# Attention value products with the values as weights, and the softmax division moved ahead of the transposes

## The reference, cut to what matters

```
# sparse attention (branch a)
logits = einsum('bqhd,bqkhd->bhqk', qb, k_sel) * scale
p = softmax(where(valid, logits, -inf))
y_a = einsum('bhqk,bqkhd->bqhd', p, v_sel)
# stick-breaking attention (branch c)
a = where(strict, exp(log_beta + later), 0.0)
y_c = einsum('bhqs,bshd->bqhd', a, v)
# every branch n, then the output
merged += gates[n] * (branches[n] @ w_branch[n])
return merged @ w_out
```

## Time and profile before

| | |
|---|---|
| median of 3 timed runs | 885.44 us (884.88 to 887.35) |
| span of the profiled execution | 883.3 us |
| outside the span (median less span) | 2.1 us |
| TensorE matmul busy | 818.1 us, 93% |
| VectorE busy | 530.9 us, 60% |
| ScalarE busy | 386.0 us, 44% |
| GpSimd busy | 119.0 us, 13% |
| DMA, mean over the span | 319 GB/s |

### The profile page before, as it was taken

One profiled execution on the slowest core, in us unless ns is written; L12 is line 12 of the kernel. 1 busy time (PEld: TensorE's weight loads), 2 busy tenths in 40 slices (PEclk: granted clock), 3 DMA queues, 4 the chain that ended last, 5 costly groups with the idle time before them and its releaser, 6 DMA issues.

```text
span 883.3 us, 20327 instructions
## 1 busy us (share of the span) xinstructions
PE 818.1 (93%) x8747; PEld 655.1 (74%) x8747; DVE 530.9 (60%) x1067; ACT 386.0 (44%) x661; POOL 119.0 (13%) x169
## 2 busy tenths in 40 slices
PE   7999999999999998876999999999999999986884
PEld 7898788888887775664589978788888876664552
DVE  5768798667545554423376788976666455544434
ACT  5646867545432222111275568674454222221113
POOL 3740101212000000000066001032200000000000
PEclk9999999999999999978999999999999999999988
DMA  9966545488979999999998464555987999999994
GB/s 303 390 227 149 187 144 189 145 366 339 385 298 419 420 418 420 420 420 421 401 368 302 150 202 134 173 173 223 402 348 273 421 420 420 418 418 420 420 420 180
DMA packets 64125, 281.47 MB, mean 319 GB/s; under 512 B 5120, under 2 KB 7248, under 8 KB 39712
## 3 DMA queue, kind: packets, MB, share of 16 engines
q1 hardware_dynamic: 62752, 278.45, 80.6%
q0 software_dynamic: 800, 1.40, 1.2%
q10 hardware_dynamic: 480, 0.28, 0.1%
HBM read 279.06 MB, written 1.05 MB: 317 GB/s over the span
## 4 chain that ended last, share of the span: by engine, by line
PE 69%; DMA 20%; SPq 5%; ACT 2%; DVE 2%; issue 1%; DVEq 0%; ACTq 0%
PE ps L492 14%; PE ps L494 14%; PE ps L493 14%; DMA ring<-in_w_exp_up 10%; PE ps L841 8%; DMA late<-in_w_exp_down 6%; PE ps L828 5%; PE ps L857 4%; DMA new_pair<-in_w_exp_up 3%; SPq L382 3%; PE ps L940 2%; SPq L396 2%; DMA ring<-in_w_in 2%; PE ps L604 1%; PE ps L847 1%
## 5 line engine op out<-in xcount | busy, mean ns | idle before, releaser
L1685 DVE TENSOR_TENSOR split_lo<-ring,split_hi 128x1024 fp32r<-128x1024 f32 (+1 forms) x142 | 198.0, 1432 | 36.1 <-ACT split_hi L1161 34.9
L492 PE MATMUL ps<-split_hi,hT_hi 128*128 128x512 f32 (+2 forms) x416 | 161.3, 388 | 3.0 <-DVE split_lo L1685 1.7
L1161 ACT ACTIVATE split_hi<-ring 128x1024 fp32r<-128x1024 f32 (+1 forms) x144 | 145.9, 1048 | 32.8 <-PE ps L494 29.8
L493 PE MATMUL ps<-split_lo,hT_hi 128*128 128x512 f32 (+2 forms) x416 | 157.6, 379 | 0.0
L494 PE MATMUL ps<-split_hi,hT_lo 128*128 128x512 f32 (+2 forms) x384 | 145.3, 378 | 0.0
L2105 DVE TENSOR_TENSOR wsT<-mb,ps 32x64 f32<-32x64 f32 x256 | 54.8, 214 | 142.3 <-ACT mb L1368 139.7
L1368 ACT ACTIVATE mb<-ps 128x64 f32<-128x64 f32 x64 | 14.3, 223 | 238.5 <-PE ps L841 238.5
L492 PEld LDWEIGHTS ps<-split_hi,hT_hi 128*128 128x128 f32 x416 | 78.2, 188 | 20.6 <-DVE split_lo L1685 3.8
L493 PEld LDWEIGHTS ps<-split_lo,hT_hi 128*128 128x128 f32 x416 | 78.4, 188 | 12.7
L494 PEld LDWEIGHTS ps<-split_hi,hT_lo 128*128 128x128 f32 x384 | 72.2, 188 | 13.2
L1589 POOL TENSOR_TENSOR idx<-idx,wt 128x128 f32<-128x128 f32 x32 | 12.1, 399 | 388.2 <-PE ps L863 306.3
(11 more groups left out here) (276 smaller groups left out, 1311.8 us busy)
## 6 DMA issues: line engine op xcount, KB each, us to landing
ring<-in_w_in SPq DMA_DIRECT2D x52, 1024.0 KB, 10.4
ring<-in_w_exp_gate SPq DMA_DIRECT2D x45, 1024.0 KB, 24.0
ring<-in_w_exp_up SPq DMA_DIRECT2D x45, 1024.0 KB, 26.0
late<-in_w_exp_down SPq DMA_DIRECT2D x38, 1024.0 KB, 26.3
ring<-in_w_exp_down SPq DMA_DIRECT2D x15, 1024.0 KB, 26.6
new_pair<-in_w_exp_gate SPq DMA_DIRECT2D x10, 1024.0 KB, 18.2
new_pair<-in_w_exp_up SPq DMA_DIRECT2D x10, 1024.0 KB, 20.3
late<-in_w_exp_gate SPq DMA_DIRECT2D x9, 1024.0 KB, 24.4
```

The lines of the kernel that those rows point to most:

```text
L492: mm(dst, st[0], mv[0], start=start, stop=False, skip_group_check=True)
L493: mm(dst, st[0], mv[1], start=False, stop=False, skip_group_check=True)
L1161: A(half_view(split_hi[:, v % SPLITS, :], v), raw_half(v, l), ACT.Copy).then_inc(hi_done, 1)
L1685: V.tensor_tensor(half_view(split_lo[:, v % SPLITS, :], v), raw_half(v, l), half_view(split_hi[:, v % SPLITS, :], v).bitcast(F32), ALU.sub ...
```

## The change

The value product is turned around. The values' 64 columns of a head become the weights, and the transposed probabilities (128 tokens) the moving operand. The result has the head's 64 columns in partitions and tokens in the free dimension, which is what the branch product needs. Heads 2k and 2k+1 go to the lower and upper 64 partitions, so consecutive products use different column halves of the array. The result needs no copy to tokens-in-partitions form and no `y_transposes`; `yT_high` reads the bank that `pv` wrote. The softmax division can no longer be done per token on the result, so a new `softmax_scale` on VectorE divides the probabilities before `p_transposes`. TensorE's order also changes: `p_transposes(zc, 0, 6)` stands behind one more half of unit 14, `p_transposes(zc, 1, 4)` behind the second half of unit 16, and `pv(vc, 1, 7)` behind `wide_unit(17)`. Some banks change, and `sparse_logits` reads two separate banks with two instructions. What is left out of the diff are the lists of semaphores and their counts.

```
@@ -578,13 +578,12 @@
                             if t == TT - 1 and c == XT_GROUPS[XT_GROUP_OF[c]][-1]:
                                 ins.then_inc(xT_mm, 1)
 
-                    def logits(qk, t, b0, done):
-
+                    def logits(qk, t, banks, done):
 
                         w = P * (t + 1)
                         for m in range(2):
                             for r in range(2):
-                                ins = mm(ps[:, b0 + r, 256 * m:256 * m + w],
+                                ins = mm(ps[:, banks[r], 256 * m:256 * m + w],
                                          qk[HD * r:HD * r + HD, m, P * t:P * t + P],
                                          qk[HD * r:HD * r + HD, 2 + m, 0:w], start=(m == 0), stop=True,
                                          skip_group_check=True)
...
@@ -599,11 +598,13 @@
 
                     def pv(v, t, b0):
 
-                        for s_, h in enumerate((0, 2, 1, 3)):
+                        for k in range(2):
                             for b in range(t + 1):
-                                ins = mm(ps[:, b0, HD * h:HD * h + HD], pT[:, b, s_, :],
-                                         v[:, b, HD * h:HD * h + HD], start=(b == 0), stop=(b == t),
-                                         skip_group_check=True)
+                                for r in range(2):
+                                    h = 2 * k + r
+                                    ins = mm(ps[HD * r:HD * r + HD, b0, T * k + P * t:T * k + P * t + P],
+                                             v[:, b, HD * h:HD * h + HD], pT[:, b, 2 * r + k, :],
+                                             start=(b == 0), stop=(b == t), skip_group_check=True)
                         ins.then_inc(pv_mm, 1)
 
                     def y_transposes(y, b0):
...
@@ -676,21 +677,22 @@
                     in_unit(7, 3, "mixed")
                     pe.wait_ge(*L(rel_out, 2))
                     emptied(2)
-                    logits(qkT_c, 0, 6, zc_mm)
+                    logits(qkT_c, 0, (6, 7), zc_mm)
                     in_unit(8, 4, "transposed")
                     in_unit(9, 4, "transposed")
                     pe.wait_ge(*L(qk_out, 1))
-                    logits(qkT_c, 1, 4, zc_mm)
+                    logits(qkT_c, 1, (4, 5), zc_mm)
                     in_unit(10, 5)
                     in_unit(11, 5)
 
                     pe.wait_ge(*L(yT_lo_out, 1))
                     wide_unit(12, 6, y_tile(0), True, True)
                     in_unit(13, 8)
+                    in_half(28, 8)
                     pe.wait_ge(*L(zexp, 1))
                     pe.wait_ge(*L(zc_out, 1))
                     p_transposes(zc, 0, 6)
-                    in_unit(14, 8)
+                    in_half(29, 8)
                     pe.wait_ge(*L(pT_out, 1))
                     pv(vc, 0, 7)
                     in_unit(15, 9)
...
@@ -700,39 +702,33 @@
                                  start=(g == 0), stop=True, skip_group_check=True)
                     ins.then_inc(sgu_mm, 1)
                     in_half(32, 9)
-                    pe.wait_ge(*L(zexp, 2))
-                    p_transposes(zc, 1, 4)
                     pe.wait_ge(*L(yb_done, 1))
                     y_transposes(y_ab, 6)
                     in_half(33, 9)
-                    pe.wait_ge(*L(pT_out, 2))
-                    pe.wait_ge(*L(y_out, 1))
-                    pv(vc, 1, 7)
+                    pe.wait_ge(*L(zexp, 2))
+                    p_transposes(zc, 1, 4)
                     pe.wait_ge(*L(yT_lo_out, 2))
                     wide_unit(17, 10, y_tile(1), True, True)
-                    pe.wait_ge(*L(y_out, 2))
-                    y_transposes(y_c, 5)
-                    logits(qkT_a, 0, 6, la_mm)
+                    pe.wait_ge(*L(pT_out, 2))
+                    pv(vc, 1, 7)
+                    logits(qkT_a, 0, (5, 6), la_mm)
                     in_unit(18, 12)
                     pe.wait_ge(*L(yT_lo_out, 3))
-                    logits(qkT_a, 1, 4, la_mm)
+                    logits(qkT_a, 1, (4, 7), la_mm)
                     in_unit(19, 12)
                     in_unit(20, 13)
-                    pe.wait_ge(*L(la_exp, 1))
+                    pe.wait_ge(*L(p_ok, 1))
                     p_transposes(sc, 0, 6)
                     in_unit(21, 13)
                     pe.wait_ge(*L(pT_out, 3))
-                    pv(vi, 0, 7)
-                    pe.wait_ge(*L(la_exp, 2))
-                    p_transposes(zc, 1, 4)
+                    pv(vi, 0, 5)
+                    pe.wait_ge(*L(p_ok, 2))
+                    p_transposes(zc, 1, 6)
                     wide_unit(22, 14, y_tile(0), True, True)
                     in_unit(23, 16)
                     pe.wait_ge(*L(pT_out, 4))
-                    pe.wait_ge(*L(y_out, 3))
-                    pv(vi, 1, 7)
+                    pv(vi, 1, 5)
                     in_unit(24, 16)
-                    pe.wait_ge(*L(y_out, 4))
-                    y_transposes(y_ab, 6)
                     in_unit(25, 17)
                     in_unit(26, 17)
                     pe.wait_ge(*L(yT_lo_out, 4))
...
@@ -1177,8 +1173,8 @@
                                 ins = A(hT_hi[:, c, :], ps[:, XT_BANK[g], at:at + T], ACT.Copy, scale=g1_col(l, c))
                             ins.then_inc(xT_hi, 1)
 
-                    def yT_high(k, at, b0):
-                        act.wait_ge(*L(yT_mm, k))
+                    def yT_high(made, at, b0):
+                        act.wait_ge(*made)
                         A(yT_hi[:, at, :, :], ps[:, b0, :], ACT.Copy).then_inc(yT_hi_out, 1)
 
                     def p_evac(k, t, b0):
...
@@ -1288,15 +1284,15 @@
                     hi_half(34, l)
                     stick_exp(1)
                     token_evac(8, sig, 0, ACT.Sigmoid)
+                    yT_high(L(yT_mm, 1), 1, 6)
+                    hi_half(35, l)
                     p_evac(2, 1, 4)
-                    yT_high(1, 1, 6)
-                    hi_half(35, l)
                     act.wait_ge(*L(gate_prod, 1))
                     token_evac(9, sig, 2, ACT.Sigmoid)
                     hi(18)
                     act.wait_ge(*L(gate_prod, 2))
                     block_evac(10, br[:, 0, :, :], 0)
-                    yT_high(2, 0, 5)
+                    yT_high(L(pv_mm, 2), 0, 7)
                     block_evac(11, br[:, 1, :, :], 2)
                     hi(19)
                     hi(20)
...
@@ -1310,7 +1306,7 @@
                     token_evac(13, sig, 2, ACT.Sigmoid)
                     hi(23)
                     act.wait_ge(*L(pv_mm, 3))
-                    p_evac(4, 1, 4)
+                    p_evac(4, 1, 6)
                     act.wait_ge(*L(gate_prod, 4))
                     block_evac(14, br[:, 0, :, :], 0)
                     block_evac(15, br[:, 1, :, :], 2)
...
@@ -1319,7 +1315,7 @@
                     act.wait_ge(*L(gate_sum, 2))
                     token_evac(16, sig, 0, ACT.Sigmoid)
                     hi(26)
-                    yT_high(3, 1, 6)
+                    yT_high(L(pv_mm, 4), 1, 5)
                     hi(27)
                     act.wait_ge(*L(gate_sum, 3))
                     token_evac(17, sig, 2, ACT.Sigmoid)
...
@@ -1818,40 +1814,27 @@
                                                          ALU.add, ALU.mult)
                         ins.then_inc(yb_done, 1)
 
-                    def y_evac_c(t):
-                        dve.wait_ge(*L(pv_mm, t + 1))
-                        V.tensor_copy(y_c[:, t, :], ps[:, 7, 0:BW]).then_inc(y_out, 1)
-
-                    def sparse_logits(t, b0, buf):
+                    def sparse_logits(t, banks, buf):
                         w = P * (t + 1)
                         m = mb[:, 0:P] if t == 0 else mb[:, P:]
                         dve.wait_ge(*L(la_mm, t + 1))
-                        link(V.tensor_tensor(buf[:, :, 0:w],
-                                             ps[:, b0:b0 + 2, :].rearrange("p b n -> p (b n)")
-                                             .rearrange("p (h s) -> p h s", h=NH)[:, :, 0:w],
-                                             m.rearrange("p (o s) -> p o s", o=1).broadcast_to([P, NH, w]),
-                                             ALU.add))
+                        for r in range(2):
+                            ins = V.tensor_tensor(buf[:, 2 * r:2 * r + 2, 0:w],
+                                                  bank(banks[r]).rearrange("p (h s) -> p h s", h=2)[:, :, 0:w],
+                                                  m.rearrange("p (o s) -> p o s", o=1).broadcast_to([P, 2, w]),
+                                                  ALU.add)
+                        link(ins)
                         link(V.tensor_reduce(lmax, buf[:, :, 0:w], AX.X, ALU.max))
-                        if t == 1:
-                            dve.wait_ge(*L(la_exp, 1))
-
-                            link(V.reciprocal(scal[:, 52:56], lsum))
```

(34 more changed lines are left out.)

69 lines of the change are left out of this document (30 added, 39 removed).

## The result

| | before | changed |
|---|---|---|
| median of 4 timed runs | 885.34 us | 889.14 us |
| span of the profiled execution | 883.3 us | 887.4 us |
| mixer of layer 0, index products to router transposes | 187.2 us | 188.1 us |
| mixer of layer 1, the same | 187.0 us | 187.8 us |
| experts of layer 0, to the first input transposes of layer 1 | 208.8 us | 209.9 us |

The changed kernel is 0.39% slower: the ratio is 1.0039, with a 95% interval of 1.0025 to 1.0053. The stages in the table are differences between the first starts of the named instructions. Their start moves by up to 1.5 us between executions, so stages are compared, not clock times. The forecast of 887.6 us had the sign and the place right and was 1.5 us short. In the profiled execution the time is 1.8 us above its span (889.17 against 887.4), not 2.1.

The account below looks back on a forecast made before the run. TensorE was taken as the bound, VectorE close behind at 81%. Per layer +2.15 - 0.64 - 0.44 = +1.07 us, +2.1 in all on the median of 885.44, gave 887.6 us; range 883.2 to 891.4.

Parts of the forecast that it names:

- The value products: On TensorE, packing in two column groups: sixteen take 1.06 us, a gain of 0.64; eight take 0.64, a gain of 0.2.
- The moved transposes: First probability transposes 1.76 us later delay VectorE's chain: half 33 cannot start before 115.8, some 2.5 us of new waiting.
- `token_evac(9)` behind `p_evac(2)`: In wide_unit(17), ScalarE frees banks 2 and 3 at 121.9, TensorE wants them at 120.9: new wait of 1.0 us.
- Half 43: Sparse branch: softmax_scale ahead of lo(21) and GpSimd's moved addition make TensorE 2.15 us late at half 43.
- The mixer's sum: Each layer's mixer: +2.15 - 0.64 - 0.44 = +1.07 us, +2.1 us in all.
- The first rival: Softmax scaling hidden by more slack at half 43: -0.05 us a layer, 885.3 us; chance 0.20.
- the second: VectorE's chain doesn't hold half 33, new waits don't come: gain of 3.5 us a layer, 878.3 us; chance 0.12.
- the third: No packing of the value products: sixteen cost 1.91 us, 2.8 us a layer slower, 891.0 us; chance 0.10.
- a rival of its own: TensorE's clock falls to the 1.2 GHz level from new waits: 1.9 us a layer on top, 891.4 us; chance 0.12.
- One to one through the experts: Experts' loads wait for VectorE's splits, which follow TensorE: a mixer ending d later shifts the end by about d.

Follow-up runs that it names:

- Run 3: Changed kernel with the value products' loops turned so all products of the lower 64 partitions come before those of the upper: 889.56 us, ratio 1.0049.
- Run 1: Changed kernel with p_transposes(zc, 0, 6) back ahead of half 28: 884.26 us, ratio 0.9991 to the kernel before.
- Run 6: Kernel of Run 1 with token_evac(9) ahead of p_evac(2) on ScalarE, 881.81 us; then also gate(2) behind lo(21) on VectorE, 880.44 us.
- Run 4: Changed kernel without the division of the probabilities for t = 0: 1495 us, with extra expert passes; only layer 0's mixer was read.
- e10_same: The changed kernel again, unaltered: 888.95 us, ratio 1.0033 to the kernel before.
- Run 2: Kernel before with ten unused 128x128 products ahead of pv(vi, 1), a delay of 2.2 us a layer: 888.70 us, ratio 1.0041.
- e6_all: Kernel of Run 1 with token_evac(9) ahead of p_evac(2) on ScalarE and gate(2) behind lo(21) on VectorE: 880.44 us, ratio 0.9944.
- e9_fill: Changed kernel with fourteen unused instructions on TensorE ahead of the wait for yb_done: 886.63 us, ratio 1.0008 to the kernel before.

## Why the prediction was right, point by point

- **The value products.** 1.06 us was forecast for sixteen and 1.02 was measured; 0.64 for eight and 0.59 (103.10 to 103.69). Within a group they start 0.055 apart, so sixteen are 0.88 and eight 0.44: on top of that come 0.14 and 0.15, where I had taken 0.21 from the `logits`. The Trainium skill's rule in "TensorE: Matmul & The Clock Gate", section "The mechanism", that weight loads overlap running products only for different row groups, would have given 1.7 by my reckoning. The traces disagree: every product here uses all rows, each weight load takes 0.13 to 0.14 us, and the products still start 0.055 apart. Run 3 shows that packing carries 0.49 of the 0.68 gained. The rest came even without packing, which I hadn't allowed for: I held that an unpacked swap costs as much as before.
- **The moved transposes.** `stick_logits(1)` 1.76 us later, measured 1.71; half 33 at 115.8, measured 115.81; idle ahead of `stick_logits(1)` 4.6, measured 4.45; the waits for `yb_done` and half 33 together 2.5, measured 2.0 from modelled ends. Run 1 shows it by taking the move back. VectorE's own shift at half 33 was 1.38 (114.54 against 113.16), 1.43 forecast.
- **`token_evac(9)` behind `p_evac(2)`.** 1.0 us forecast, 0.90 measured. Run 6 shows that the order on ScalarE is the whole cause.
- **Half 43.** 2.15 us late forecast, 2.12 measured (149.70 against 147.58). Run 4 shows VectorE's part. Run 6 takes away two things at once, the 1.2 us of `gate(2)` ahead of `lo(21)` and the hold by GpSimd (`lo(21)` takes 2.35 us instead of 4.56), so it doesn't tell GpSimd's part by itself.
- **The mixer's sum.** +1.07 a layer forecast, +0.9 and +0.8 measured. The first rival (the scaling is hidden) falls with run 4, the second (VectorE's chain doesn't hold) and the third (no packing) with the traces.
- **The term that was missing is the clock.** The sum had none of it: I kept it as a rival of its own with a chance of 0.12 and a price of 1.9 us in each layer, on top of the forecast, and didn't let it happen in some executions and one layer only. Behind the wait for `yb_done` it measured 1.6 us, in layer 0, in three of four traces. In `e10_same` this stands in the span: 2.6 and 0.8 us from the mixers, 1.0 and 0.6 from the experts and the last stretch, less 0.6 at the start, together 4.4. It can't be what lifted the first trace of the changed kernel, 889.17 us, where that fall is absent; there 1.7 us are the mixers' and 2.2 lie behind them. So the forecast came near for the reason it gave, but the 1.5 us it was short by are not one term in every execution.
- **One to one through the experts.** Run 2 fits it: 4.4 us added, 3.6 to 3.9 measured. The prediction left out that the clock can also fall behind the mixer. The experts of layer 0 take 209.8 to 209.9 us in three traces (the changed kernel twice, and `e4_no_scale0`) and 208.8 to 209.1 in the other seven. These three, and no others, have 3.4 us at the 1.2 GHz level behind a wait of 2.5 to 2.6 us for `late<-in_w_exp_up`, where the others waited 0.2 to 1.5. So the difference of about 1 us in layer 0's experts is that fall. The two traces of the changed kernel have it at the same place of layer 1 (around 866 us), but the last stretch, 218.4 to 219.7 us, isn't ordered by it alone: `e6_all` takes 219.4 without it. Why the fall comes in three of the five traces with the wait for `yb_done` (`e3_serial` and `e9_fill` are spared) and in none of the five without it stays open.

## What to carry to other kernels

When an instruction is moved behind other work to hide a wait, list who waits for that instruction on the other engines, and follow each of them down to the next thing that the bound engine needs. Here 0.9 us of TensorE's time was saved and VectorE's chain came 1.4 us later, with 0.93 of slack. An added operation on an engine that is 81% busy costs nothing only where its chain has slack; here a reordering of two neighbours on ScalarE and two on VectorE gave back about 4 us (ratio 0.9991 to 0.9944; the mixers 4.3 shorter). If a wait of a microsecond or two on TensorE can't be removed, try filling it with unused products: here 2.0 us of waiting were followed by a fall of the clock that cost 1.6.

## What the runs showed of the hardware that was not expected

- The granted clock fell to the 1.2 GHz level for 3.4 us after two waits of 1.57 and 0.47 us with a little work between them, inside a stage that otherwise kept TensorE busy. It did so in three traces of four, in the same place. In the same kernel filled with fourteen unused instructions it did not, though TensorE still waited 0.47 us.
- At the end of layer 0's experts the load of the last weights landed at the same time (197.8 to 198.2 us behind the router transposes, in all ten traces). The 64 products on them took 3.2 to 3.6 us where the clock had fallen and 1.9 to 2.3 where it hadn't.
- Sixteen float32 products with 64 weight columns and 128 moving columns, most of them on the same column half, took 1.51 us, 0.094 each. The same number with 128 weight columns and 64 moving ones took 0.106, so turning the shapes around, without alternating the halves, gave a tenth. Which of the two sizes it comes from wasn't tried.
- A VectorE operation with both inputs in SBUF and a GpSimd addition held each other up, and in the two cases here the one that began first wasn't slowed, as far as the rows tell. In `e6_all` the scaling began 0.04 us after the addition, took 3.44 us instead of 1.22 and ended 1.08 us behind it (146.92 against 145.84), while the addition took 2.40. In the changed kernel the addition began 0.16 us into the first split of `lo(21)` and took 3.32; the second split ended 1.08 us behind it (149.64 against 148.56).
